# Layer norm applied before the first expert routing instead of after its gathers

## What is computed

```python
h_l = rms_norm_2(lat, norm2_w[layer]) * (1.0 + mod_l[4]) + mod_l[3]
lat = lat + mod_l[5] * expert_choice_ffn(h_l, moe_router[layer], ...)
if keep_ctx:                       # the first of the two layers only
    h_c = rms_norm_2(cx, norm2_w[layer]) * (1.0 + mod_c[4]) + mod_c[3]
    cx = cx + mod_c[5] * expert_choice_ffn(h_c, ...)

def expert_choice_ffn(h, router_w, w_gate, w_up, w_down):
    aff = softmax(h @ router_w)
    gate, idx = top_k(swapaxes(aff, 1, 2), cap)
    xe = h[idx]                    # the gathered tokens of each expert
    a, u = xe @ w_gate, xe @ w_up
    ye = (silu(a) * u) @ w_down * gate[..., None]
    return zeros.at[idx].add(ye)
```

## Times and profile before

| | |
|---|---|
| timed runs | 2656.27, 2661.17, 2662.34 us (median 2661.17) |
| profiled execution | 2658.91 us, of it a span of 2656.3 us |
| TensorE busy | 2468.3 us (93%) |
| VectorE busy | 1125.2 us (42%) |
| ScalarE busy | 759.8 us (29%) |
| POOL busy | 51.6 us (2%) |
| transfers | 570.46 MB, mean 215 GB/s |
| first routing | 1219.6 to 1295.6 us of the span |
| experts, layer 0 | from 1295.6 us on |

### The profile page before, as it was taken

How to read it: one execution, slowest core, us unless ns; L and a number is a source line. 1 busy time by engine, 2 the same in 40 slices (tenths; PEclk the granted TensorE clock), 3 DMA queues, 4 the chain that set the end, 5 groups by cost and what they waited for, 6 DMA issues and landing times. The chain is left out here.

```text
span 2656.3 us, 39271 instructions
## 1 busy us (share of the span) xinstructions
PE 2468.3 (93%) x16684; PEld 1535.0 (58%) x16684; DVE 1125.2 (42%) x2210; ACT 759.8 (29%) x1586; POOL 51.6 (2%) x68
## 2 busy tenths in 40 slices
PE   8989999999899999978799999997999969988887
PEld 7856888888677778765433434343767743322222
DVE  5455633333787878786200000002556542211113
ACT  4345433332532222213311111112347522111002
POOL 0000000000000000000200000000000010000000
PEclk9989999999999999988899999999999979999999
DMA  5231322222210101025899999997240469999996
GB/s 204 106 144 67 132 89 99 95 101 101 78 50 33 50 32 50 32 111 206 329 384 385 383 390 382 389 382 297 101 159 2 191 253 363 428 428 428 428 428 280
DMA packets 58101, 570.46 MB, mean 215 GB/s; under 512 B 6815, under 2 KB 15015, under 8 KB 24776
## 3 DMA queue, kind: packets, MB, share of 16 engines
q1 hardware_dynamic: 50904, 544.37, 51.3%
q0 software_dynamic: 5584, 18.35, 2.2%
q10 hardware_dynamic: 1440, 5.24, 0.5%
HBM read 554.84 MB, written 13.11 MB: 214 GB/s over the span
## 5 line engine op out<-in xcount | busy, mean ns | idle before, releaser
L2922 PE MATMUL moe_gate<-ring,moe_xe_l 128*32 128x512 f32 (+1 forms) x1240 | 192.0, 598 | 18.0 <-DMA ring<-in_moe_gu 12.2
L3906 DVE SCALAR_TENSOR_TENSOR moe_hidden<-moe_hidden,moe_gate_rows,moe_up 128x512 f32<-128x512 f32 x31 | 23.2, 748 | 400.1 <-ACT moe_hidden L3829 400.1
L2922 PE MATMUL moe_up<-ring,moe_xe_l 128*32 128x512 f32 (+1 forms) x1240 | 189.9, 594 | 0.0
L3934 DVE SCALAR_TENSOR_TENSOR residual<-experts_psc,mod,residual 128x512 f32<-128x512 f32 (+1 forms) x78 | 54.8, 708 | 305.9 <-PE experts_psc L3770 169.8
L3690 PE MATMUL experts_py_l<-ring,experts_turn_l 128*32 128x512 f32 (+1 forms) x1136 | 142.0, 596 | 3.8 <-DMA ring<-in_moe_down 3.1
L1019 DVE TENSOR_TENSOR mlp_w_lo<-ring,mlp_w_hi 128x512 fp32r<-128x512 f32 x144 | 96.7, 689 | 97.7 <-ACT mlp_w_hi L964 97.4
L3829 ACT ACTIVATE moe_hidden<-moe_gate 128x512 f32<-128x512 f32 x31 | 18.5, 597 | 361.3 <-PE moe_up L2922 361.3
L964 ACT CAST mlp_w_hi<-ring 128x512 fp32r<-128x512 f32 x144 | 86.4, 618 | 123.3 <-PE mlp_acc L920 123.3
L2922 PEld LDWEIGHTS moe_up<-ring,moe_xe_l 128*32 128x32 f32 (+1 forms) x1240 | 49.5, 115 | 107.7 <-issue 107.7
L2922 PEld LDWEIGHTS moe_gate<-ring,moe_xe_l 128*32 128x32 f32 (+1 forms) x1240 | 44.6, 115 | 100.7 <-issue 69.5
L918 PE MATMUL mlp_acc<-mlp_h_hi,mlp_w_hi 128*128 128x512 f32 x256 | 100.0, 391 | 0.0
(11 more groups left out here) (658 smaller groups left out, 5099.7 us busy)
## 6 DMA issues: line engine op xcount, KB each, us to landing
ring<-in_moe_gu SPq DMA_DIRECT2D x91, 2048.0 KB, 11.1
ring<-in_moe_down SPq DMA_DIRECT2D x45, 2048.0 KB, 10.0
ring<-in_ada_w SPq DMA_DIRECT2D x24, 2048.0 KB, 7.8
ahead_wide_early<-in_moe_gu SPq DMA_DIRECT2D x9, 2048.0 KB, 30.5
ahead_wide_high<-in_moe_gu SPq DMA_DIRECT2D x9, 2048.0 KB, 30.5
ahead_wide_low<-in_moe_gu SPq DMA_DIRECT2D x9, 2048.0 KB, 30.4
normed<-in_moe_gu SPq DMA_DIRECT2D x9, 2048.0 KB, 30.5
ring<-in_w_up SPq DMA_DIRECT2D x8, 2048.0 KB, 7.8
```

The costliest lines, as they stand in the source:

```text
L2922: last = core.nc.tensor.matmul(banks[m][at:at + n, :], xe_l[:, e, k, a:a + n], columns(2 * kk + m, FH * half, FH), start=(k == 0), stop=(k ...
```

## The change

The first routing (with context) gets a function of its own, `route_both`; the second keeps `route_stage`. Against `route_stage`, `route_both` differs as follows.

- It opens with `TokenScaling`: `rstd` is spread (six tiles), VectorE scales the residual into `core.h` (16 operations), and ScalarE adds the shift in place (16 operations). The router products read `core.h`, feature tile by feature tile as each is ready. Folded gain, shift sums and the operations on the scores go.
- Token rows are turned from `core.h`, so the rows in DRAM are whole, and each half of a gathered group is copied in one operation of 128x512.
- Modulation chunks 0 and 1 run ahead of the scores, 2 to 4 ahead of the turned places, and only 5 behind the lists.
- SP issues the first expert chunk as before and then waits for the sixth gather (`landed[2]`) before it issues the second and third.
- The stores of the two context tiles count on a semaphore of their own, which POOL also waits for.

```diff
+                scaling.gains(dve)
+                for k in range(KD):
+                    scaling.scale(dve, k)
...
+                for k in range(KD):
+                    act.wait_ge(scaling.scaled.handle, scaling.scaled.at(k + 1))
+                    for c0, n, g, sc, sh in streams:
+                        last = nc.scalar.activation(core.h[:, k, c0:c0 + n], core.h[:, k, c0:c0 + n], ACT.Identity, bias=sh[:, k:k + 1])
+                    last.then_inc(normed.handle, 1)
+                    if k == 1 and MOD_OPEN[layer]:
+                        part.keep_row(act, 0)
...
+                scaling.spread_columns(pe)
+                for i in range(MOD_OPEN[layer]):
+                    part.step(pe, i)
...
+                    pe.wait_ge(normed.handle, normed.at(k + 1))
+                    for c0, n in spans:
+                        last = nc.tensor.matmul(pr[q:q + 32, c0:c0 + n], core.routers[:, k].rearrange("p l e -> p (l e)"), core.h[:, k, c0:c0 + n], start=(k < 4), stop=(k >= 4), tile_position=(0, q))
+                    if k == 3:
+                        turn_half(0)
+                    if k == 5:
+                        turn_half(1)
...
+                for i in range(2, 6):
...
+                if ctx:
+                    core.stream(sp, part.n0 + part.n - 2)
+                    sp.wait_ge(landed[2].handle, landed[2].at(16 * land.count(2)))
+                    core.stream(sp, core.used)
...
+                    dst, src = keep(j, 0)
+                    nc.scalar.copy(dst, src).then_inc(kept[0].handle, 1)
...
+                    dst, src = keep(j, 1)
+                    nc.vector.tensor_copy(dst, src).then_inc(kept[1].handle, 1)
...
-        pick_l = route_stage(core, layer, ctx, streams, gate_up, hidden, xe_l, xe_c, sp_l, sp_c, slots_l, gate_rows, gate_c, wide, ada)
+        pick_l = (route_both if ctx else route_stage)(core, layer, ctx, streams, gate_up, hidden, xe_l, xe_c, sp_l, sp_c, slots_l, gate_rows, gate_c, wide, ada)
```

More of the change, by code:

```diff
@@ L2981, in route_stage @@
         tok_kept = st.counter("route_tok_kept", len(halves))
-        tok_stored = st.counter("stored", 16 * tiles)
+        late_rows = 2 if ctx else 0
+        tok_stored = st.counter("stored", 16 * (tiles - late_rows))
+        late_stored = st.counter("ex_silu_done_l", 16 * late_rows) if ctx else None
         numbered = st.counter("route_cleared", 1)
@@ L3022, in _ @@
                 if ctx:
+                    core.stream(sp, part.n0 + 1)
+                    sp.wait_ge(tok_stored.handle, tok_stored.at(16 * (tiles - late_rows)))
+                    core.stream(sp, part.n0 + part.n - 2)
+                    sp.wait_ge(landed[2].handle, landed[2].at(16 * land.count(2)))
                     core.stream(sp, core.used)
@@ L3041, in _ @@
                 nc.gpsimd.memset(one[0:W, :], 1.0).then_inc(cleared.handle, 1)
-                pool.wait_ge(tok_stored.handle, tok_stored.at(16 * tiles))
+                pool.wait_ge(tok_stored.handle, tok_stored.at(16 * (tiles - late_rows)))
+                if ctx:
+                    pool.wait_ge(late_stored.handle, late_stored.at(16 * late_rows))
                 for j in range(len(groups)):
@@ L3203, in store @@
                     act.wait_ge(tok_kept.handle, tok_kept.at(max(i for i, half in enumerate(halves) if half[0] == t) + 1))
-                    act.dma_start(core.token_rows[t * P:(t + 1) * P, :], tok[:, t] if t < LT else tok_ctx[:, t - LT]).then_inc(tok_stored.handle, 16)
+                    act.dma_start(core.token_rows[t * P:(t + 1) * P, :], tok[:, t] if t < LT else tok_ctx[:, t - LT]).then_inc((tok_stored if t < tiles - late_rows else late_stored).handle, 16)
                 nc.scalar.activation(warm[:], core.ones[0:1, :], ACT.Exp)
```

369 lines of the change are left out of this document (added).

## The result

| | before | after |
|---|---|---|
| median of the timed runs | 2658.98 us (22 runs) | 2662.52 us (22 runs) |
| profiled execution | 2658.91 us, span 2656.3 us | 2662.34 us, span 2660.6 us |
| first routing, first instruction to first expert product | 76.0 us | 82.3 us |
| gathers, first issue to last landing | 26.3 us | 31.5 us |

The ratio of the two kernels' times is 1.0019, with a 95% interval from 1.0012 to 1.0027: the changed kernel is 5.0 us slower (3.2 to 7.2), just under the 0.2% (5.3 us) that the prediction took for the least it could tell from no change. The ratio goes by all runs; the two medians alone lie 3.5 us apart. The forecast was 2662.6.

What follows compares the result with a forecast made beforehand. TensorE is busy for most of the span, so a change is worth what it takes from its stage's length. +2.65 us at the first gather and +0.25 behind it, +2.9 on the 2659.7 average: 2662.6 us, range 2654 to 2669.

Steps and rivals of the forecast that it cites:

- the bounds of the sum: Whole change: +2.9 us, between +1 (early first gather, last pair warm) and +5 (late gather, cold, slow copies).
- Opening: Routing start to scores: scaling and shifting in place ends the scores +8.9 us; removed work leaves +7.55 us at the softmax.
- The slower rival, a cold opening: TensorE's clock stays low in the opening: scores at about 1239, experts +8 us, 2667.5 us; chance 0.22.
- Softmax and top-k: Scores to index: top-k as long as before, TensorE 1.2 us late to the places instead of 1.9; index +6.85 us.
- Stores: Token-row stores end at about 1260, no longer gate the gathers, hiding 4.2 us; first gather +2.65 us.
- Gathers and the wait: First gather to last landing: SP's wait gives undisturbed first gathers, then chunks take most bytes; last lands some 5 us later.
- The last pair: Turning the last gathered pair before the experts takes 2.4 to 3.9 us; 2.5 us was taken.
- Copies: Copies behind the gathers: one for four takes 0.7 us; 8 to 9 us saved is spent waiting for bytes.
- After the stage: Experts onward: the expert stage is paced by its products and moves as a whole; second routing untouched.
- The gathers keep their speed: Faster rival: gathers get half the bandwidth beside the chunks, experts 3 to 4 us before today; middle 2653; chance 0.18.
- The wait is idle, or it costs: SP's wait binds; without it experts come some 5 us earlier, near 2657 us; counted inside the 0.60 case.
- the main case: The summed forecast of a small slowdown in the first routing, 2657 to 2666 us; chance 0.60.

Runs made afterwards that it cites:

- e8: e7 with token halves 0 and 1 turned behind the router products instead of between them; ratio 0.9976 to the kernel before.
- e7: e5 with ScalarE's load of the exp table moved ahead of the shifts; ratio 0.9984 to the kernel before.
- e4: The changed kernel with each half of a gathered group copied in four plain pieces again; ratio 1.0020 to the kernel before.
- e10: The kernel before with only the first routing's copies made whole, gain and shift of gathered tokens left out; ratio 0.9992 to the kernel before.
- e5: The changed kernel with chunk two no longer held and chunk three held until the twelfth gather; median 2651.57 us, ratio 0.9972 to the kernel before.
- e3: The changed kernel with both expert chunks held until the twelfth gather instead of the sixth; ratio 1.0003 to the kernel before.
- e9: The changed kernel with chunks two and three each loaded by four DMAs of 4 KB per partition instead of one of 16 KB; median 2656.98 us.
- e1: The changed kernel without SP's wait for the sixth gather; median 2657.35 us, ratio 0.9995 to the kernel before.

## Why the prediction was right, and which of its terms were not

**Direction and size.** The direction was right. That the median came out 0.1 us from the number is luck: the lead grew by 6.2 us and not by 2.9, and the forecast stood on the average of four executions, 2659.7, which is 0.7 us above the median of 22. The measured +5.0 us lies at the upper edge of the bounds of the sum, +1 to +5. The 3.3 us of lead that the sum lacked are +0.5 at the first gather, +3.1 from there to the last landing, and -0.3 behind it.

**Opening: the sum right, by two errors.** Sixteen scales took 8.61 us (I took 9.2). ScalarE did not stop for chunk 0's product, whose first run took 2.62 us at a clock of 0.61: the product was done at 1226.65, and ScalarE was at its second step until 1226.83. So the shifts ended 12.2 us after the start and not 13.2. But the scores ended 2.4 us behind them and not 1.2, with a token half between the last products; e8, without it, has 0.9 us less. Scores: +9.2 us (predicted +8.9). The slower rival, a cold opening, did not come: the granted clock rose to 1.00 for 1226.7 to 1232.7.

**Softmax and top-k: one error each way.** The -1.35 us of removed work was there (softmax +7.9), but the top-k began 8.9 us later than before: VectorE waited 1.79 us for the affinities where it had waited 0.71. I had asked whether TensorE is late to the places and not whether it is late to the affinities, and I had priced nothing there at the low clock, which is what the four halves ran at (e7 and e8). At the places it was on time, where I had taken 1.2 us. Index: +7.3 (predicted +6.85).

**Stores: right.** The last store landed at 1262.7 (I said about 1260), before the index. First gather +3.2 us (predicted +2.65; bounds +1.55 to +3.75).

**Gathers and the wait: the mechanism right, its size short by 3.1 us.** This is the term that was mis-sized. Last landing 31.5 us after the first issue, and I said 28.4. Of the sum's steps:
- the sixth gather landed 6.4 us after issue, not 4.7. My row was one gather alone; with one issued each 1.25 us the time to landing grew from 4.5 us for the first to 6.4 for the sixth to ninth. In 1272 to 1280 the queue moved 330 GB/s and not 411, and only gathers were in it;
- the chunks' data flowed 3.2 us after SP's issue, not 1.8, so the stretch shared with them began later;
- the shares were as taken: 41 packets against 44, 82 to 18% of the bytes (85 to 15% in the earlier trace rows);
- the last 4.2 us moved 187 GB/s, and in 1.6 us of them it was 26 GB/s. The sum had every byte at 411 GB/s until the last one.

**The last pair: 3.67 us, not 2.5.** TensorE had been idle for 4.61 us before it, and the granted clock over the turns was 0.50. The prediction's 2.4 to 3.9 us had this end, and I took the other one: 1.2 us. It did not lengthen the sum, since I also had the last pair wait 1.5 us for the turning of the pair before it, which was long done. From the last landing to the experts it was 4.7 us, and I had 5.0.

**Copies: right.** 0.59 us on ScalarE and 0.69 us on VectorE (0.7 taken), covered by the bytes, and e4 shows that four pieces cost nothing there. The prediction's "8 to 9 us is spent waiting for bytes" is what e10 shows for the kernel before as well, but for 1.8 us.

**After the stage: that it moves as a whole is not refuted.** From the first expert product to the start of the attention stage passed 566.6 us in the kernel before (1295.62 to 1862.18) and 563.8 us in the changed one:

```profile
1867.25 2.90 PE L439 MATMUL w_in_acc<-ident,norm_col 128*128 128x128 f32 x12 [0.97 <-PEq L4061]
```

TensorE's waits there fell from 4.3 to 1.4 us for weights and from 9.5 to 8.2 us for `token_sums`. That looks as if 2.8 us of the lead had been given back. But e4, with the changed kernel's transfers and its lead, took 566.8 us over the same stretch, and e5 and e7, alike in both, took 564.1 and 568.5 us: single executions differ by more than what is to be explained. Over all thirteen changed kernels the time by the ratios (ratio minus 1, times 2659) follows the lead one for one: a line through them and the kernel before has 1.0 us of time for each microsecond of lead, and the kernels lie 2.2 us off that (standard deviation). The largest exception is e3, 5.0 us off: its stretch took 568.2 us, with 5.5 us of waits for weights. There a shorter lead was in part given back.

**The rivals.** "The gathers keep their speed" fell with the share. Its condition, a share of about half, is what e9 makes: that brought 8.0 us of lead, 1.7 us less than the kernel before has, where the rival had 3 to 4. "The wait is idle, or it costs": it costs. I had put the kernel without it at about 2657 for 5 us less to the experts, and e1 measured 2657.35 with 7.6 us less. The prediction treated this as an aside within the main case; it was the whole result, since without the wait the change is worth nothing measurable either way.

## What to carry to other kernels

When two queues feed one deadline, write down which bytes are needed first and let the others start either well before or behind them. A wait that let the bulk loads in while the last urgent transfers were under way was the worst of the places tried: it cost 7.6 us of lead, and moved by one chunk and six gathers it became a gain (ratio 0.9972). Before you price a wait, compare packet sizes of the two queues: here the one with the larger packets took the bandwidth, and cutting its transfers into rows of 4 KB was worth 8 us of lead without touching the order.

## What the runs showed of the hardware

- Two queues on the same DMA engines took turns packet by packet to within a few per cent (41 and 44, 110 and 108, 172 and 172), for packets of 16 KB against rows of 4 KB as well as for equal ones. The chunks' packets were as large as a partition's row of the transfer (16 KB, or 4 KB when cut).
- Gathers of 512 KB, issued one each 1.25 us with no chunk beside them, landed 4.5 us after issue for the first and 6.4 us for the sixth to ninth (changed kernel; 4.6 and 6.8 to 6.9 in e9). Beside the chunks it was up to 17.5 us.
- In the kernel before, where the first two gathers landed 11.0 and 12.1 us after issue, POOL stood still for 5.44 us ahead of its eighth gather though it waited on no semaphore there, and issued it 0.5 us after the second one had landed. e10 shows the same (5.41 us, and again 0.5 us); the changed kernel, whose second gather had landed in time, has no such pause. Chunks beside the first gathers thus also delay the issue of the later ones.
- Data of SP's loads began to flow 1.0 us after the issue into a nearly idle queue (chunk two of the kernel before, issued at 1261.04) and 3.2 us after it beside a full queue of gathers (changed kernel).
- The last gather behind a mixed stretch ended at the pace of one DMA engine in sixteen: 1.6 us at 26 GB/s. e4 shows such an end too (1294.9 to 1295.9 at 37 GB/s, share 0.09). Why one engine is left behind is open; I made no run on it.
- In e7 and in the changed kernel TensorE's granted clock fell to 0.57 and 0.61 right behind a stretch of 2.5 us in which it had worked for 1.34 us. In e8 it worked for 2.28 of 2.4 us there and kept 1.00. Turning the same four halves took 3.37 us in e7 and 1.94 us in e8.
